# Final RMSNorm of a decoder trunk: smaller root groups, three row tiles shared with GpSimd, last down products in PSUM banks 0 and 1

## The reference, cut to what matters

```python
def _rmsnorm(x, g):
    x32 = x.astype(jnp.float32)
    y = x32 * lax.rsqrt(jnp.mean(x32 * x32, axis=-1, keepdims=True) + EPS)
    return (y * g.astype(jnp.float32)).astype(x.dtype)
...
        hid = jax.nn.silu(jnp.einsum('td,edf->tef', ht, w_gate[o])) * jnp.einsum('td,edf->tef', ht, w_up[o])
        out = out + jnp.einsum('tef,efd->td', hid * c_o[:, :, None], w_down[o])
...
    return _rmsnorm(x, final_g)
```

## Time and profile before

| | |
|---|---|
| median of 3 runs | 1058.49 us |
| the three runs | 1055.88, 1058.87, 1058.49 us |
| the profiled execution | 1059.06 us |
| its span, from the first to the last instruction | 1057.0 us |
| around the span | 2.06 us |
| TensorE, VectorE, ScalarE, GpSimd busy over the span | 94%, 46%, 26%, 14% |
| TensorE's mean granted clock | 0.971 of full speed |

### The profile page before, as it was taken

The page is one execution under the profiler, slowest core; times in us unless marked ns, Lnnn a source line. Parts: engine busy times, 40 slices in busy tenths (PEclk is TensorE's granted clock), DMA queues, the critical chain, the costliest instruction groups (busy, mean ns, idle before and its releaser), DMA issues. The chain is left out here.

```text
span 1057.0 us, 13460 instructions
## 1 busy us (share of the span) xinstructions
PE 990.6 (94%) x5091; PEld 578.5 (55%) x5091; DVE 488.7 (46%) x1221; ACT 276.4 (26%) x621; POOL 150.2 (14%) x146
## 2 busy tenths in 40 slices
PE   6999999999999899999999999996999997999991
PEld 4435787766555466666667455555454333444440
DVE  3496390386645377666665124264652111211125
ACT  3201111301223476566655111020001000101024
POOL 3000000131211221110010000011121221212230
PEclk9999999999999899999999999995999999999996
DMA  9310240133300560000000242657689999999965
GB/s 266 111 37 4 81 80 0 19 28 102 79 1 1 127 199 2 1 2 2 1 1 2 79 153 103 237 204 293 241 300 359 356 393 396 391 392 396 387 220 228
DMA packets 61744, 165.79 MB, mean 157 GB/s; under 512 B 32747, under 2 KB 34859, under 8 KB 49319
## 3 DMA queue, kind: packets, MB, share of 16 engines
q1 hardware_dynamic: 53296, 145.99, 38.4%
q0 software_dynamic: 8096, 18.42, 6.8%
q10 hardware_dynamic: 288, 0.53, 0.1%
HBM read 147.41 MB, written 25.24 MB: 163 GB/s over the span
## 5 line engine op out<-in xcount | busy, mean ns | idle before, releaser
L2011 PE MATMUL banks<-shared,wout 128*64 128x512 f32 (+1 forms) x352 | 125.5, 612 | 6.5 <-issue 4.8
L1621 PE MATMUL banks<-wout,shared 128*128 128x512 f32 x256 | 112.7, 594 | 0.5 <-PEq L1276 0.5
L1324 ACT ACTIVATE shared<-shared,low 128x640 f32<-128x640 f32 (+7 forms) x128 | 92.9, 729 | 3.5 <-DVE low L1411 3.1
L2059 DVE SCALAR_TENSOR_TENSOR mix_bt<-mix_bt,slot_coef,banks 128x256 f32<-128x256 f32 x24 | 11.5, 480 | 161.8 <-ACT mix_bt L2039 161.7
L385 PE MATMUL banks<-x,wout 128*128 128x512 f32 x192 | 84.6, 595 | 0.8 <-DVE x L426 0.8
L2011 PEld LDWEIGHTS banks<-shared,wout 128*64 128x64 f32 (+1 forms) x352 | 47.2, 166 | 68.3 <-issue 67.8
L1374 PE MATMUL banks<-consts,shared 128*128 128x128 f32 x528 | 79.2, 286 | 2.0 <-ACT shared L1324 1.2
L1374 PEld LDWEIGHTS banks<-consts,shared 128*128 128x128 f32 x528 | 56.9, 142 | 41.7 <-issue 36.9
L1621 PEld LDWEIGHTS banks<-wout,shared 128*128 128x128 f32 x256 | 47.6, 190 | 55.2 <-issue 55.2
L1356 PE MATMUL banks<-shared 64*128 64x512 f32 (+3 forms) x384 | 72.0, 492 | 1.9 <-PEq L995 1.3
L1411 DVE CUSTOM_DVE_ANT_0 shared<-banks,bias 128x640 f32<-128x640 f32 (+4 forms) x96 | 52.7, 598 | 39.1 <-PE banks L1356 38.9
(11 more groups left out here) (366 smaller groups left out, 1342.6 us busy)
## 6 DMA issues: line engine op xcount, KB each, us to landing
shared<-in_exp_w_down SPq DMA_DIRECT2D x22, 1024.0 KB, 21.9
shared<-in_exp_w_gate SPq DMA_DIRECT2D x22, 1024.0 KB, 13.4
shared<-in_exp_w_up SPq DMA_DIRECT2D x22, 1024.0 KB, 18.6
x<-in_exp_w_down SPq DMA_DIRECT2D x10, 1024.0 KB, 29.0
x<-in_exp_w_gate SPq DMA_DIRECT2D x5, 1024.0 KB, 25.3
x<-in_exp_w_up SPq DMA_DIRECT2D x5, 1024.0 KB, 30.5
late<-in_exp_w_up SPq DMA_DIRECT2D x5, 1024.0 KB, 23.9
late<-in_exp_w_gate SPq DMA_DIRECT2D x5, 1024.0 KB, 16.6
```

The costliest lines, as they stand in the source:

```text
L1324: nc.scalar.activation(prob[:, u % 2, at:at + n], prob[:, u % 2, at:at + n], ACT.Exp, bias=low[:, u % 2, v, j:j + 1], scale=-1.0, accum_ou ...
L1621: ins = nc.tensor.matmul(psum[n % 4], src[:, i * P:i * P + P], m["wout"][:, k, half * 512:half * 512 + 512], start=k == 0, stop=k == KD - 1)
L2011: ins = nc.tensor.matmul(psum[2 + p][rows].rearrange("p (a f) -> p a f", a=2), xt[:, p, k, rows], wgu[b][:, :, k], start=k == 0, stop=k == ...
```

## The change

Four groups of columns take the place of three: tiles 0 and 1, tiles 2 and 3, tiles 4 to 7, the z tiles. ScalarE takes the roots of tiles 0 and 1, and with them the table load, before it squares tile 2. VectorE inverts group 0 and scales tiles 0 and 1 ahead of its first sum, then tile 3 between the two sums, then tiles 5 and 7, then the z tiles. GpSimd multiplies tiles 2, 4 and 6 by `final_g`; ScalarE scales 2 and 4; tile 6 is scaled by a second GpSimd instruction, a `tensor_scalar` with `rstd` per row, after tile 5 is done on VectorE. The stores follow in the order 0, 1, 3, 2, 5, 7, 4, 6. The last pass's down products go to banks 0 and 1, so that they no longer wait for the first sum. In the branch for overflow tiles, which this input does not take, the inverses are formed by the new groups.

```diff
--- before.py
+++ after.py
@@ -1944,11 +1944,11 @@
     homes = ([wgu[0].rearrange("p a k f -> p (a k f)")[:, i * D:i * D + D] for i in range(4)]
              + [wd[0][:, i] for i in range(2)] + [m["spare"][:, i * D:i * D + D] for i in range(2)])
     by_square = [("x", i) for i in range(NT)] + [("z", i) for i in range(DIRECT)]
-    by_norm = [("x", i) for i in range(2, NT)] + [("z", i) for i in range(DIRECT)]
-    shared_tiles = (0, 1)
-    store_order = (2, 3, 4, 0, 5, 1, 6, 7)
+    by_norm = [("x", i) for i in (0, 1, 3, 5, 7)] + [("z", i) for i in range(DIRECT)]
+    shared_tiles = (2, 4, 6)
+    store_order = (0, 1, 3, 2, 5, 7, 4, 6)
     gained, scaled = sem("rows_gained"), sem("rows_scaled")
-    groups = [slice(0, 4), slice(4, 8), slice(8, 10)]
+    groups = [slice(0, 2), slice(2, 4), slice(4, 8), slice(8, 10)]
     nth_norm = {what: k + 1 for k, what in enumerate(by_norm)}
     column = {what: slice(k, k + 1) for k, what in enumerate(by_square)}
 
@@ -2020,7 +2020,10 @@
                                       hid[:, p, :].rearrange("p (q k) -> p k q", k=2)[:, k], m["ident"])
         ins.then_inc(s["h_t"], 1)
 
-    def pe_down(pe, n, bufs, p, wait):
+    def y_bank(n):
+        return 0 if n == NP - 1 else 6
+
+    def pe_down(pe, n, bufs, p, wait, bank=6):
         pe.wait_ge(s["h_out"], n + 1)
         if wait:
             pe.wait_ge(s["y_act"], n)
@@ -2030,7 +2033,7 @@
             for k in range(2):
                 for v, b in enumerate(bufs):
                     rows = slice(v * w, v * w + w)
-                    ins = nc.tensor.matmul(psum[6 + part][rows], hidt[:, p, k, rows], wd[b][:, k, part * 512:part * 512 + 512],
+                    ins = nc.tensor.matmul(psum[bank + part][rows], hidt[:, p, k, rows], wd[b][:, k, part * 512:part * 512 + 512],
                                            start=k == 0, stop=k == 1)
         ins.then_inc(s["y_done"], 1)
 
@@ -2071,7 +2074,7 @@
         dve.wait_ge(stored[n % 2], rows_out(n))
         for part, done in enumerate(("y_act", "y_dve")):
             cols = slice(part * 512, part * 512 + 512)
-            V.tensor_tensor(y[:, n % 2, cols], xg[:, n % UN, cols], psum[6 + part], ALU.add).then_inc(s[done], 1)
+            V.tensor_tensor(y[:, n % 2, cols], xg[:, n % UN, cols], psum[y_bank(n) + part], ALU.add).then_inc(s[done], 1)
 
     def act_square(act, what, at, again=0):
         kind, i = what
@@ -2148,8 +2151,10 @@
             for i in range(NT):
                 sp.dma_start(homes[i], last_rows[i]).then_inc(last_in[i][0], 16)
             for i in store_order:
-                if i in shared_tiles:
-                    sp.wait_ge(scaled, i - shared_tiles[0] + 1)
+                if i == shared_tiles[-1]:
+                    sp.wait_ge(gained, len(shared_tiles) + 1)
+                elif i in shared_tiles:
+                    sp.wait_ge(scaled, shared_tiles.index(i) + 1)
                 else:
                     sp.wait_ge(o_done, nth_norm["x", i])
                 sp.dma_start(out_rows[i], homes[i]).then_inc(out_stored, 16)
@@ -2192,6 +2197,9 @@
             for i in shared_tiles:
                 gp.wait_ge(ss_done, column["x", i].stop)
                 nc.gpsimd.tensor_tensor(homes[i], homes[i], m["fg"], ALU.mult).then_inc(gained, 1)
+            gp.wait_ge(o_done, nth_norm["x", 5])
+            gp.wait_ge(gained, len(shared_tiles))
+            nc.gpsimd.tensor_scalar(homes[6], homes[6], rstd[:, column["x", 6]], None, ALU.mult).then_inc(gained, 1)
             for i in range(DIRECT):
                 put_out(gp, i)
 
@@ -2228,8 +2236,11 @@
 
             def scaled_tile(i, known):
                 act.wait_ge(o_done, nth_norm[known])
-                act.wait_ge(gained, i - shared_tiles[0] + 1)
+                act.wait_ge(gained, shared_tiles.index(i) + 1)
                 nc.scalar.mul(homes[i], homes[i], rstd[:, column["x", i]]).then_inc(scaled, 1)
+
+            def roots(g):
+                act_roots(act, groups[g], groups[g].stop)
 
             for n in range(first):
                 act_gate(act, n, n % 2)
@@ -2241,15 +2252,18 @@
             squares((0,))
             act_gate(act, first + 1, (first + 1) % 2)
             act_hid(act, first, first % 2)
-            squares((1, 2, 3))
+            squares((1,))
+            roots(0)
+            squares((2,))
             act_hid(act, first + 1, (first + 1) % 2)
-            act_roots(act, groups[0], 4)
+            squares((3,))
+            roots(1)
             squares((4, 5, 6, 7))
-            act_roots(act, groups[1], 8)
+            roots(2)
+            scaled_tile(2, ("x", 3))
             squares((8, 9))
-            act_roots(act, groups[2], 10)
-            for i in shared_tiles:
-                scaled_tile(i, ("x", 2))
+            roots(3)
+            scaled_tile(4, ("x", 5))
 
             def over_tile(k):
                 act_gate(act, k + NP, 0)
@@ -2290,7 +2304,7 @@
             def down(n):
                 for j in passes[n][1]:
                     pe.wait_ge(wd_in[buffer_of(j)], 16 * nth[j])
-                pe_down(pe, n, [buffer_of(j) for j in passes[n][1]], n % 2, n > 0)
+                pe_down(pe, n, [buffer_of(j) for j in passes[n][1]], n % 2, 0 < n < NP - 1, y_bank(n))
 
             for n in range(first):
                 up(n)
@@ -2463,15 +2477,17 @@
             for n in range(first, NP):
                 dve_hid(dve, n, passes[n][0], n % 2)
             dve.wait_ge(fg_in, 16)
+            inverses(0)
+            for i in (0, 1):
+                dve_scaled(("x", i))
             dve_sum(dve, first)
-            inverses(0)
-            for i in (2, 3):
+            inverses(1)
+            dve_scaled(("x", 3))
+            dve_sum(dve, first + 1)
+            inverses(2)
+            for i in (5, 7):
                 dve_scaled(("x", i))
-            dve_sum(dve, first + 1)
-            inverses(1)
-            for i in (4, 5, 6, 7):
-                dve_scaled(("x", i))
-            inverses(2)
+            inverses(3)
             for i in range(DIRECT):
                 dve_scaled(("z", i))
 
@@ -2482,9 +2498,8 @@
 
             def all_again(extra):
                 dve.wait_ge(root_done, len(groups) + 1)
-                for h in range(2):
-                    four = slice(4 * h, 4 * h + 4)
-                    inverse_root(nc, chain, rstd[:, four], root[:, four], ss[:, four], newton)
+                for g in groups[0:3]:
+                    inverse_root(nc, chain, rstd[:, g], root[:, g], ss[:, g], newton)
                 for i in range(NT):
                     dve_scaled(("x", i))
```

## The result

The changed kernel takes 1061.79 us (median of 16 runs, 1059.74 to 1065.51), the kernel before 1058.67 (16 runs, 1055.88 to 1060.57). The ratio is 1.0026 with the interval 1.0013 to 1.0038, so about 2.8 us slower: beyond the scatter, as the interval leaves out 1, and inside the 0.3% that the prediction called no change. Its 1060.6 is 1.2 us under the median.

What follows compares the result with a forecast made beforehand. The last unbroken run of stores was taken to bound the end. Unhindered engines gave 2.65 us earlier, but VectorE and GpSimd taking turns on SBUF gave 2.1 later: 1058.49 + 2.1 = 1060.6 us, range 1055.6 to 1062.9.

Steps and rivals of the forecast that it cites:

- What bounds the end: End section: the last unbroken run of stores sets the end, followed by a fixed 6.8 us of two indirect writes.
- the rule of a run of stores: Last unbroken run of n stores: landing = issue of its first + 1.3 + 1.3 n us.
- Step by step, if each engine kept its pace: Final scalings and stores without interference: tile 5's store begins the last run at 1041.0, landing 1047.5, 2.65 us earlier.
- What the engines do to each other: VectorE beside GpSimd: with two SBUF operands against GpSimd's reads, one waits the other's full time; the other bound was 0.
- The sum with turns taken: End section with VectorE and GpSimd alternating: last run from 1045.75, landing 1052.25, 2.1 us later; chance 0.69.
- the signs named beforehand: Trace: tile 1's scaling about 2 us late, inverse product about 2.3, GpSimd products over 3, last landing near 1052.3.
- The table load: ScalarE: the load is moved ahead, not added, takes 1.28 us, and the root starts 0.01 after it.
- Rival C: ScalarE: a second table load returns after the first root, two loads costing 2.6 us but no kernel time; chance 0.03.
- The banks: TensorE's last down products: the 1.30 us wait on the sum goes, worth 0 because VectorE's queue covers it.
- rival B: GpSimd's second pass over tile 6: dear `tensor_scalar`, 4.7 us makes it 3.9 later, 1062.4; chance 0.20 with worse turns.
- Its deciding point: GpSimd's second pass over tile 6 decides the end once it takes more than 2.9 us (1046.8 to 1049.6).
- Rival A: VectorE and GpSimd do not hinder each other at this width: 2.65 us earlier, 1055.8; chance 0.11.

Runs made afterwards that it cites:

- run 1: The changed kernel without GpSimd's three products and its second pass over tile 6; 1054.24 us.
- run 5: The changed kernel with only tile 1 shared with GpSimd, scaled by ScalarE, and no second pass; 1056.49 us, ratio 0.9978 to the kernel before.
- run 6: The changed kernel with all eight x tiles on VectorE, none scaled by GpSimd or ScalarE; 1057.14 us, ratio 0.9986 to the kernel before.
- run 9: The changed kernel with only tile 0 shared with GpSimd, squared first, and no second pass; 1054.96 us, ratio 0.9969 to the kernel before.
- run 10: The kernel with only tile 0 shared, plus two extra GpSimd `tensor_scalar` of 128x1024 while VectorE is nearly idle; span 1053.0 us, instructions 2.87 and 2.84.
- run 2: The changed kernel with each of GpSimd's three products replaced by three memsets of the same tile; 1058.07 us.
- run 8: The kernel before with only the last down products moved to banks 0 and 1; 1058.57 us, ratio 1.0.
- run 7: The changed kernel with the last down products back in banks 6 and 7, waiting for the sum; 1065.9 us, ratio 1.0057 to the kernel before.
- run 3: The changed kernel with tile 6's second GpSimd pass as a two-operand product instead of `tensor_scalar`; 1062.23 us.
- run 4: The kernel before with GpSimd's product of tile 1 held until the first root, beside VectorE's inverse; 1061.26 us.

## Why the prediction was right, point by point

- **What bounds the end**: held. The last landing follows the rule of a run of stores to 0.06 us in the changed kernel, and the 6.8 us of indirect writes behind it (1057.9 - 1051.0 = 6.9) stayed. As what delays the run lies in VectorE's queue, runs 1, 5, 6 and 9 moved the end by removing collisions there.
- **Step by step, if each engine kept its pace** (2.65 earlier): run 1 comes closest to this case, and gave 36.1 - 33.0 = 3.1 earlier, with tile 5's store no longer late. It has no GpSimd pass at all; by an estimate, one of 2.85 us (run 10) behind tile 5, done there at 1038.98, would have had tile 6 ready at 1041.8, ahead of its place in the run of stores (1043.7), so it would not have moved the end. The first root came at 1028.60, forecast 1030.35 - 1.53 = 1028.82.
- **What the engines do to each other**: held at the width for which there was no row. It was the choice between 0 and the other instruction's full time; runs 1 and 2 separate them. The Trainium skill ("SBUF — State Buffer", section "Who interferes with whom") states the same for two SBUF operands against a GpSimd instruction that reads; the scalings of 3.46 and 3.38 agree, and the memset run agrees for an instruction that only writes. The same section says that `tensor_scalar`, where its operands allow it, can take both pairs of ports and then contend, which I had passed over: 0.45 and 0.56 beside memsets, 0.82, 1.12 and 1.86 beside reading instructions agree. So of the inverse's six steps not three can be held, as I wrote, but at least five.
- **The sum with turns taken** (2.1 later): the total is near (2.4), the order of turns in it was not, so that the total is right in part by luck. Two of its terms are also short: GpSimd's products of tiles 2 and 4 are put 2.0 and 2.05 behind the scaling that each waits for (1032.8 to 1034.8, 1036.0 to 1038.05), though a product was priced at 2.35. With 2.35 in both, the sum says 2.7 and not 2.1. I let VectorE win the first near tie. It started at 1029.77, GpSimd at 1029.80, and GpSimd's product went through first (2.36), so that VectorE's tile 0 ended at 1033.2 where I had 1031.3. GpSimd stayed a turn ahead, and by then had its third product beside the two sums, which are not hindered. Of the 2.3 us that I charged to an inverse product only 1.12 was left, and it fell on `tensor_scalar`. A loss of 1.9 at tile 0 and 2.0 at tile 1 and the first sum shrank to 0.3 at inverse 1 (1039.66 against 1040.9 - 1.53 = 1039.37), and to 0.2 at tile 5's store (1044.44 against 1044.22). In this trace each product delays VectorE once, whichever goes first: 2.2, 2.1 and, where the PSUM sum covers part of it, 0.95 us. Of the signs named beforehand, tile 5's store and the last landing (1051.00 against 1052.3 - 1.53) came. Tile 1's scaling was to end about 2 us after where 1.2 us each would put it and ended 4.4 after (1036.53 against 1032.17). The inverse product of 2.3 us did not come, and of GpSimd's products (2.36, 2.60, 3.33) only the third reads over 3 us.
- **The table load**: moved, one only, 1.28 us, with the root 0.01 behind it. Rival C did not occur. Squares 4 to 7 and the copy ran after the first root without a load.
- **The banks**: worth 0 against the kernel before (run 8), and the cover named, VectorE's queue, is the right one as long as the new banks are there. What I did not price is the other half: with turns taken, the old banks would have cost 2.1 us of tail (run 7), since the sum that frees them is late. Without them the ratio is 1.0057 and not 1.0026.
- **The new instruction, rival B**: my upper bound failed. It takes 2.85 alone, not at most 2.35. Its deciding point was given as 2.9 us behind tile 7 (its own times, 1046.8 to 1049.6, make 2.8); there it took 1048.33 - 1045.53 = 2.8 from the point where VectorE let it start. So it stood at the deciding point, and run 3 shows that 0.94 less is worth nothing. Tile 6's store and tile 5's run end together.
- **Rival A** fell with runs 1 and 4. **The number**: 1058.49 + 2.1 = 1060.6 had two small lacks. The tail grew by 2.4 and not 2.1, and the median before is 1058.67 over more runs; 1058.67 + 2.4 = 1061.1. That the profiled execution before lay 0.57 above the median of the runs then known, and the one after 2.0 below its own, shows how little one execution's time tells of a median. The remaining 0.7 to 1061.79 is within what the interval leaves open (1.4 to 4.0 us over the kernel before).

## What to carry to other kernels

Before work goes from VectorE to GpSimd, look at when it will run: beside a VectorE instruction with two SBUF operands, or a small `tensor_scalar`, a GpSimd product of 2.4 us that reads SBUF cost VectorE up to 2.2 us here, nearly two scalings, where it was to save one; in VectorE's idle time, or beside work on PSUM, it cost nothing. Small dependent steps such as an inverse are the worst neighbours, as a step of 0.17 us can take 2.2. And where stores set the end, ask when the first of the last unbroken run is issued and how evenly the tiles come, not only when the last tile is done.

## What the runs showed of the hardware that I had not expected

- A `tensor_scalar` of VectorE on 128x2 elements with one SBUF operand waits for GpSimd as well, even for a memset that reads nothing (0.45 and 0.56 us in place of 0.17).
- GpSimd's `tensor_scalar` with a factor per row is dearer than its product of two tiles: 2.85 against 2.36 us on 128x1024.
- Beside that instruction VectorE was let go early. Its step at 1045.79 ended at 1046.60 (0.81 us, and 0.81 again in runs 2 and 7), while GpSimd's pass is recorded to 1048.33, and the first z scaling, begun at 1047.23, kept its 1.2 us beside the rest of it. Beside a two-operand product VectorE's instructions ended with it, to 0.02 us (run 4). Why, stays open, and was not tried.
- Who wins a near tie stays open too: GpSimd's product went first at 1029.80 although VectorE's scaling is recorded as started 0.03 us earlier, and so it did in runs 3 and 7, with the same 0.03.
- TensorE, idle for 7.91 us and granted 0.50, took 5.34 us for eight matmuls that take 3.67 at 1.00, and got the higher level back while they ran.
